# Moving four modulation items from the GDN heads to VectorE in the attention, with the gate's sigmoid on ScalarE

## What is computed

```python
c_act = jax.nn.silu(c)
for i in range(DEPTH):                                   # DEPTH = 2
    ada = (c_act @ ada_w[i] + ada_b[i])[:, None, :]      # 1 x 6144: six items
    sh1, sc1, g1, sh2, sc2, g2 = jnp.split(ada, 6, axis=-1)
    h = rms_norm(x) * (1.0 + sc1) + sh1
    y = gdn_mixer(h, ...) if i == 0 else fox_mixer(h, ...)
    x = x + g1 * y
    h = rms_norm(x) * (1.0 + sc2) + sh2
    x = x + g2 * hier_moe(h, ...)
return rms_norm(x, final_norm)

# fox_mixer, per head: q, k normalised; s = q k^T / 8 + cum_q - cum_k, causal
p = softmax(where(mask, s, -inf)); o = p @ v
o = o * jax.nn.sigmoid(g_out)
return o @ w_out
```

## Time and profile before

| | us |
|---|---|
| median of 3 runs (lowest, highest) | 1465.35 (1463.05, 1469.11) |
| profiled execution, its own time | 1467.78 |
| its span in the trace | 1466.2 |
| TensorE busy | 1337.1 (91% of the span) |
| VectorE, ScalarE, GpSimd busy | 731.8, 435.3, 397.0 |
| heads 1 to 6, 128.68 to 421.84 | 293.2 |
| attention, eight pairs, 854.3 to 1113.2 | 258.9 |

### The profile page before, as it was taken

One profiled execution on the slowest core, in us unless ns is written; L12 is line 12 of the kernel. 1 busy time (PEld: TensorE's weight loads), 2 busy tenths in 40 slices (PEclk: granted clock), 3 DMA queues, 4 the chain that ended last, 5 costly groups with the idle time before them and its releaser, 6 DMA issues.

```text
span 1466.2 us, 24949 instructions
## 1 busy us (share of the span) xinstructions
PE 1337.1 (91%) x9111; PEld 859.8 (59%) x9111; DVE 731.8 (50%) x1520; ACT 435.3 (30%) x1033; POOL 397.0 (27%) x588
## 2 busy tenths in 40 slices
PE   4999999999999989999886999999999979999881
PEld 2677767777775455555442777777764545555440
DVE  3656566667652466522223445666654557322224
ACT  4434424434442110000002645555541200000002
POOL 3022022112230023444334054434410024344320
PEclk8899999999999989999898899999999999999996
DMA  8255554512154279999997222122046379999995
GB/s 360 115 208 201 215 213 177 197 59 115 58 222 131 114 263 405 418 418 419 421 420 319 90 88 73 73 80 108 26 191 239 154 277 415 421 419 418 419 398 200
DMA packets 56693, 350.27 MB, mean 239 GB/s; under 512 B 18408, under 2 KB 18880, under 8 KB 30992
## 3 DMA queue, kind: packets, MB, share of 16 engines
q1 hardware_dynamic: 44992, 332.02, 57.1%
q0 software_dynamic: 11520, 16.83, 3.1%
q10 hardware_dynamic: 80, 0.04, 0.0%
HBM read 342.45 MB, written 27.34 MB: 252 GB/s over the span
## 4 chain that ended last, share of the span: by engine, by line
PE 70%; DMA 15%; DVE 9%; issue 2%; ACT 2%; POOL 1%; SPq 0%; POOLq 0%; DVEq 0%; ACTq 0%
PE PS L1116 10%; PE PS L771 8%; DMA hT<-in_moe_w_down_dram 8%; PE PS L773 7%; PE PS L772 7%; PE PS L1059 6%; PE PS L1123 5%; DMA Dr<-in_ada_w_dram 4%; PE PS L749 2%; PE PS L1143 2%; PE PS L1133 2%; PE PS L862 2%; PE PS L908 2%; PE PS L1108 2%; PE PS L1294 2%
## 5 line engine op out<-in xcount | busy, mean ns | idle before, releaser
L771 PE MATMUL PS<-hHi,Whi 128*128 128x512 f32 x512 | 225.3, 440 | 2.5 <-DVE hLo L1789 2.4
L773 PE MATMUL PS<-hHi,Wlo 128*128 128x512 f32 x512 | 202.8, 396 | 0.0
L772 PE MATMUL PS<-hLo,Whi 128*128 128x512 f32 x512 | 202.0, 394 | 0.0
L1360 ACT COPY arena<-PS 128x512 f32<-128x512 f32 (+4 forms) x256 | 108.6, 440 | 281.9 <-PE PS L862 104.7
L1116 PE MATMUL PS<-Wr,arena 128*64 128x256 f32 x1408 | 165.4, 389 | 9.8 <-DVE arena L2195 9.8
L1583 ACT ACTIVATE arena<-PS 128x128 f32<-128x128 f32 x72 | 20.0, 278 | 464.9 <-PE PS L1116 369.0
L1116 PEld LDWEIGHTS PS<-Wr,arena 128*64 128x64 f32 x1408 | 101.5, 140 | 88.8 <-issue 29.0
L2477 POOL DMA_INDIRECT y_rows<-arena x72 | 77.0, 1070 | 258.5 <-DVE arena L2207 252.2
L2418 POOL TENSOR_TENSOR Wlo<-Wr,Whi (+1 forms) x72 | 94.0, 1324 | 178.7 <-ACT Whi L1360 178.7
L771 PEld LDWEIGHTS PS<-hHi,Whi 128*128 128x128 f32 x512 | 97.6, 191 | 33.8 <-issue 18.2
L2201 DVE TENSOR_TENSOR arena<-arena,PS 128x128 f32<-128x128 f32 x72 | 20.7, 288 | 185.6 <-ACT arena L1583 169.0
(11 more groups left out here) (394 smaller groups left out, 2301.6 us busy)
## 6 DMA issues: line engine op xcount, KB each, us to landing
Wr<-in_moe_w_gate_up_dram SPq DMA_DIRECT2D x52, 2048.0 KB
Dr<-in_ada_w_dram SPq DMA_DIRECT2D x42, 1024.0 KB, 26.8
Dr<-in_moe_w_down_dram SPq DMA_DIRECT2D x28, 1024.0 KB
arena<-in_moe_w_gate_up_dram SPq DMA_DIRECT2D x14, 2048.0 KB
hT<-in_moe_w_down_dram SPq DMA_DIRECT2D x26, 1024.0 KB
Wr<-in_gdn_w_dram SPq DMA_DIRECT2D x8, 2048.0 KB, 8.6
Wr<-in_fox_w_dram SPq DMA_DIRECT2D x8, 2048.0 KB, 8.1
shift_scale<-in_moe_w_down_dram SPq DMA_DIRECT2D x12, 1024.0 KB
```

Of the source, the lines that this page charges most:

```text
L771: mm(out_ap, a_hi, b_hi, start=(k == 0), stop=False)
L772: mm(out_ap, a_hi, b_lo, start=False, stop=False)
L773: return mm(out_ap, a_lo, b_hi, start=False, stop=(k == KD - 1))
L1360: return nc.scalar.copy(dst, src)
```

## The change

`ADA_HEADS` becomes 3: two items in each of the heads 0 and 1, item 6 in head 2, item 7 in the last head. Items 8 to 11 (`LATER` = 8) are made in the attention, as eight *halves* of 512 numbers. For one half SP makes four loads of 512 KB into the part of `Dr` that the attention doesn't use, in two buffers; VectorE multiplies by `c` and adds up, in eight products over 128x512 (`later_products`); TensorE sums over the partitions in four matmuls with ones into PS[7]; VectorE adds the bias (`later_item`), and SP stores the result (`later_store`). The products of half 0 stand ahead of the attention; those of half p+1 stand in pair p, two in each query tile, the first of them ahead of the first tile's `pn_ok`. The gate is now e^(-ln(1+e^-g)), two ScalarE instructions behind the copy of v; VectorE's L2348 and L2349 are gone, and ScalarE's take of the gate doesn't wait for `sgt_ok` any more. New semaphore names stand for old semaphores that go on counting.

```diff
-ADA_HEADS = 5
+ADA_HEADS = 3
+LATER = 2 + 2 * ADA_HEADS
...
+        later_w = [Dr[:, 1, a * 1024:a * 1024 + 1024].rearrange("p (k c) -> p k c", k=2) for a in range(2)]
+        later_acc = ada_acc[:].rearrange("p i c -> p (i c)")
+        later_made = ada_bias[:, 0, 0:P]
...
@@ SP, sublayer_rows and experts
                 if layer == 1:
                     sp.wait_ge(wo_ok, WO)
+                    sp.wait_ge(later_out, 16 * 6 + later_dma_from)
...
                 if layer == 0:
+                    sp.wait_ge(ada_out[1], 16 * ADA_HEADS)
...
@@ SP, attention
+            def later_loads(m, at, quarters):
+                for q in quarters:
+                    if not isinstance(m, int) or m * KD + 2 * q - 2 > 0:
+                        sp.wait_ge(later_mul, m * KD + 2 * q - 2 + later_mul_from)
...
+                    later_load(*at, q)
...
+            def later_store(m, at):
+                sp.wait_ge(later_row, m + 1 + later_row_from)
...
+                load(later_half_row(ada_rows, *at), later_made[0:97:32, :], later_out)
+                sp.wait_ge(later_out, m * 16 + 16 + later_dma_from)
...
+            def later_step(m, at, then):
+                later_loads(m + 1, then, range(2))
+                later_store(m, at)
+                later_bias_load(then)
+                later_loads(m + 1, then, range(2, 4))
...
             bias_rows(0)
+            sp.wait_ge(modc_in, 32)
+            later_bias_load((LATER, 0))
+            later_loads(0, (LATER, 0), range(4))
             with sp.Fori(0, 3) as j:
                 for u in range(2):
                     pair_load(j * 2 + (2 + u), u, j * 2 + (1 + u))
                     bias_rows(j * 2 + (1 + u))
+                    later_step(j * 2 + u, (j + LATER, u), (j + (LATER + u), 1 - u))
             bias_rows(H - 1)
             sp.wait_ge(fpj_ps, 4 * 7)
             out_load(fox_w_out, 0, 0, mix_w[0])
+            later_step(H - 2, (11, 0), (11, 1))
             after_projection(1)
+            later_store(H - 1, (11, 1))
             sublayer_rows(1)
@@ TensorE, attend
                     pe.wait_ge(sqr_ok, p * 2 + (m + 1))
+                    if m == 0:
+                        if not isinstance(p, int) or p > 0:
+                            pe.wait_ge(later_row, p + later_row_from)
...
-                fill(2, 7)
+                fill(2, 5)
+                pe.wait_ge(fr_ok, p * 2 + 1)
+                pe.wait_ge(later_mul, p * KD + KD + later_mul_from)
+                for j in range(4):
+                    last = mm(PS[7][32 * j:32 * j + 32, 0:P], ones[:, 0:32], later_acc[:, j * P:j * P + P], start=True, stop=True)
+                last.then_inc(later_sum, 1)
+                fill(5, 7)
@@ ScalarE
-                    after(act, sgt_ok, p)
                     ins = A(eg, PS[1][:], ACT.Exp, scale=-1.0)
...
                 cp(vS.rearrange("p n c -> p (n c)"), PS[4][:]).then_inc(vs_ok, 1)
+                link(A(eg, eg, ACT.Ln, bias=one_ap))
+                after(act, on_ok, p)
+                A(sgate, eg, ACT.Exp, scale=-1.0).then_inc(sgt_ok, 1)
@@ VectorE
+            def later_products(m, k0, k1):
+                for k in range(k0, k1):
+                    if k % 2 == 0:
+                        dve.wait_ge(later_in[k // 2 % 2], m * 32 + (16 * (k // 4 + 1) + later_in_from[k // 2 % 2]))
+                    w = later_w[k // 2 % 2][:, k % 2, :]
+                    if k == 0:
+                        TS(later_acc, w, cact[:, 0:1], None, ALU.mult).then_inc(later_mul, 1)
+                    else:
+                        dve.wait_ge(later_mul, m * KD + k + later_mul_from)
+                        STT(out=later_acc, in0=w, scalar=cact[:, k:k + 1], in1=later_acc, op0=ALU.mult, op1=ALU.add).then_inc(later_mul, 1)
+            def later_item(p):
+                dve.wait_ge(later_sum, p + 1 + later_sum_from)
+                dve.wait_ge(later_bias, p * 16 + 16 + later_dma_from)
+                TT(later_made, PS[7][:, 0:P], later_made, ALU.add).then_inc(later_row, 1)
...
+                    if qt == 0:
+                        later_item(p)
+                    if more:
+                        later_products(p + 1, 2 * qt, 2 * qt + 1)
                     for a in range(2):
                         u = 2 * qt + a
                         dve.wait_ge(pr_ok, p * 8 + (u + 1))
...
+                    if more:
+                        later_products(p + 1, 2 * qt + 1, 2 * qt + 2)
                     if more and qt >= 2:
                         square_low(p + 1, qt - 2)
-                dve.wait_ge(fev, p * 4 + 4)
-                link(TS(eg, eg, 1.0, None, ALU.add))
-                nc.vector.reciprocal(sgate, eg).then_inc(sgt_ok, 1)
...
+            later_products(0, 0, KD)
             for m in range(2):
                 square_low(0, m)
             attend(0)
```

More of the change, by code:

```diff
@@ L417, in build @@
         on_ok = sem("on_ok")
+        later_in, later_in_from = (modc_in, cum_out), (32, 16)
+        later_mul, later_sum, later_row = osum_ok, sso_ps, s_ok
+        later_mul_from, later_sum_from, later_row_from = H, H, 3 * H
+        later_out, later_bias = ada_out
+        later_dma_from = 16 * ADA_HEADS
+        loop_passed = dve_passed
         r_ps, r_e, r_both, r_rank, r_pos, idx_ok = (sem(n) for n in ("r_ps", "r_e", "r_both", "r_rank", "r_pos", "idx_ok"))
@@ L564, in experts @@
                     sp.wait_ge(fs_ps, 2 * H)
+                    sp.wait_ge(later_mul, H * KD + later_mul_from)
                 for e in range(2):
@@ L576, in experts @@
                 sp.wait_ge(wo_ok, i * WO + 2 * NT)
+                if i == 1:
+                    sp.wait_ge(later_out, 16 * H + later_dma_from)
                 for g in range(2):
@@ L1699, in _ @@
             with act.Fori(0, 2) as j:
-                link.enter(j, 4)
+                link.enter(j, 6)
                 pair_step(j * 2 + 2, 0, j + 2)
@@ L2357, in _ @@
             with dve.Fori(1, H - 1) as p:
-                link.enter(p - 1, 17)
+                link.enter(p - 1, 16)
                 attend(p)
```

11 lines of the change are left out of this document (added).

## The result

| | us |
|---|---|
| before, median beside the change | 1467.23 (1463.05 to 1470.16) |
| changed kernel, median of 4 runs | 1518.83 (1513.39 to 1519.32) |
| ratio, 95% interval | 1.0332 (1.0298 to 1.0365) |
| profiled execution after, and its span | 1513.39, 1511.6 |

The account below looks back on a forecast made before the run. TensorE was taken as the bound in heads and attention; 38.6 us lost (5.5 + 0.5 + 18.5 + 9 + 0.6 + 1.5 + 3) less 16.8 gained gave +21.8, so 1487 us on the median, range 1468 to 1503.

Parts of the forecast that it names:

- the price of a loop pair: Pairs 1 to 5: VectorE's first product waits for its load, 3.7 us a pair, 18.5 in all; bounds 1.2 and 5.2.
- the start: Start of the attention: half 0's loads and eight products delay the low squares, TensorE 5.5 us late; bounds 4 and 8.
- The heads: Heads 2, 3 and 4 lose 16 matmul groups: 16.8 us gained, or 14.4 if load waits come up again.
- Pair 6: The load of half 7 stands behind 2 MB of `fox_w_out`: 9 us lost, bounds 7 and 11.
- The clock behind the two long stalls: Start and pair 6: the clock may fall to 1.2 GHz behind them, 3 us together, bounds 0 and 4.
- `modq`: Behind the last pair: its load waits for the last half's store, 1.5 us lost, bounds 0 and 4.
- The 3.5 us stalls I take as too short.: Pairs' first-tile stalls: claimed too short to lower TensorE's clock, so no clock loss was counted there.
- rival (c): Every stall lowers the clock, 2 us more in five pairs, and longer chains: 1497 to 1503 us, chance 0.14.
- I take 0.3 a pair.: TensorE's four sums over the partitions in each pair: 0.2 to 0.4 us, taken as 0.3.
- I give them 0.2 us a pair, for the third one.: VectorE's seven products behind the first in a pair: 0.2 us, for the third, whose tile has little slack.
- rival (d): Products take 1.77 us beside GpSimd, 9 us more over pairs 1 to 6: 1496 us, chance 0.08.
- it lands at 932.5: Pair 2: the first load, behind bias rows issued at 927.65, lands at 932.5; VectorE waits 2.2 us.

Follow-up runs that it names:

- e4: The kernel before with only the gate's sigmoid moved to ScalarE, no item moved: 1466.9 us, ratio 0.9995.
- e3: The changed kernel with three unread matmuls ahead of TensorE's first-tile wait in every pair: 1515.0 us, ratio 1.0307.
- e8: The changed kernel with half 0's loads issued ahead of the cumulative sums and its products split round VectorE's copy: 1512.1 us, ratio 1.0329.
- e10: The changed kernel with loads early, products moved into VectorE's idle time, each half's second load behind the pairs' weights: 1461.9 us, 0.9959 of the kernel before.

## Why the prediction was wrong

The step that failed is the price of a loop pair: 3.7 us forecast, with bounds of 1.2 and 5.2, and 7.5 measured, 19 of the 23.6 us by which the sum of this execution was short. Its largest part is the clock behind the pairs' stalls, which the prediction put at nothing. The second is the start, 5.5 forecast and 11.3 measured. The path itself was right.

**What held.** The bound and the mechanism: TensorE waits for VectorE in the first tile, and VectorE for a load of `Dr` that goes out behind the bias rows. The heads (15.9 us in heads 1 to 7, forecast 16.8). The bias rows go out 6.84 us behind the weights (930.74 against 923.90), the forecast's 927.65 - 920.64 = 7.01. VectorE has the item done at 933.91, 9.3 us into the pair, where the forecast had 8.9. ScalarE's gate at no cost (e4). Pair 6: TensorE idle for 8.21 us and 10.4 lost, forecast 9 and a share of the clock. The clock behind the two long stalls: TensorE worked 3.2 and 3.8 us at 0.50 behind them, which loses 3.5, forecast 3. The last pair, 0.4 against 0.6. `modq`, put at 1.5, cost nothing that the trace shows: TensorE's first instruction behind the last pair had no wait. The 1.1 us behind it lie within the 351.1 to 354.2 that this stretch took in all these traces.

**What failed.**

1. *"The 3.5 us stalls I take as too short."* The stalls came out at 4.0 to 4.3 us, and behind each TensorE worked at half clock, for 3.4 us or, in pair 4, 4.9. This cost 1.9 us a pair in the mean (1.8 by e3): 9.3 of the 23.6 us. It was rival (c), whose price of 2 us was right and whose chance was put at 0.14. The rows gave no ground for "too short". The 4 us of the earlier trace rows are the length of the window, and the wait in that place was 5.25:

```profile
758.39 1.03 PE L1143 MATMUL PS<-Dr,arena 128*32 128x512 f32 x1 [5.25 <-DMA hT<-in_moe_w_down_dram]
```

   That said what one longer wait does and nothing about 3.5. In e3 the clock fell even in pairs where TensorE's last idle stretch was only 1.64 and 1.81 us.
2. *The start, "5.5 us".* It was 11.3. The forecast had the first load there 4.9 us after the bias rows' issue, and then two more round trips of 3.3 us. In the trace the first product runs 6.85 us after that issue (834.46 against 827.61), the third pair of products at 840.57, some 4.3 us after the products that free its buffer, and the last pair at 845.18. Its load went out at about 838.1, the end of the first four products, and took 7.0 us: right behind it, at 839.07, SP sent the 2 MB of weights, which the forecast had nowhere beside it. The first load's 1.9 us and the last one's 3.7 make up nearly all of the difference of 5.8. That the last is due to the weights is not shown by a run made for it. It fits e8, where the same quarter has no weights right behind it and lands after 5.2.
3. *TensorE's sums: "I take 0.3 a pair."* By e10 a pair in which nothing is late is 0.93 us longer than before, so this was 0.6 too little, 3 us over the five pairs.
4. *"I give them 0.2 us a pair, for the third one."* TensorE waited 0.64 to 0.79 there. In pairs 2, 4 and 5 the product ahead of that tile's reciprocals takes 1.84 us instead of 0.75 (949.35), while GpSimd makes a low half at the same time:

```profile
949.36 1.29 POOL L2510 TENSOR_TENSOR Wlo<-Wr,Whi  x1 [4.87 <-ACT Whi L1428]
951.15 1.28 POOL L2510 TENSOR_TENSOR Wlo<-Wr,Whi  x1 [0.50 <-ACT Whi L1428]
```

   The scaling behind it, at 951.30, takes 1.34, where the next one takes 0.42 (952.75). In pairs 1 and 3 the product stays at 0.75, and both scalings are stretched in its place, with the same wait for TensorE. In pair 1:

```profile
908.77 0.75 DVE L2402 SCALAR_TENSOR_TENSOR ada_acc<-Dr,cact,ada_acc 128x512 f32<-128x512 f32 x1
909.63 1.26 DVE L2436 TENSOR_SCALAR arena<-arena 128x384 f32<-128x384 f32 x1
911.00 1.37 DVE L2436 TENSOR_SCALAR arena<-arena 128x384 f32<-128x384 f32 x1
```

   So a product there delays the tile by more than its own 0.75, whichever instruction GpSimd's work falls on. In the kernel before the first of these scalings took 0.95 already. This is rival (d) in one of its places. In the other place, the first product, it holds in part: 0.95 to 1.11 us in pairs 1 to 3, 0.48 and 0.49 in pairs 4 and 5. And the 1.77 us of the earlier trace rows, which the prediction called the far bound, is the median of L2320. The Trainium skill, GPSIMD Engine Reference, Specifications, names contention with GpSimd for instructions of VectorE with two SBUF inputs, which the product is. The trace agrees for it, with 1.84 against 0.75. The scaling has only one tensor as input and is stretched as well. That sentence of the skill also names a two-port mode, and no run here tells whether it applies.
5. *The first load of a pair, "it lands at 932.5".* That is 4.85 us after the bias rows' issue; the product that needs it started 6.1 us after it in pair 2 (936.86 against 930.74) and 7.0 in pairs 4 and 5, so 1.3 to 2.1 us later than forecast. The forecast's 3.5 held 0.3 of TensorE's own sums and started from the 0.17 of before, so a wait of 3.4; TensorE waited 4.1 in the mean. The price came from the earlier trace rows, where no other large load was issued close by. SP also needs 0.6 to 0.7 us to issue one such load (1.46 for two, at 931.44), against 0.34 for the bias rows.

By pair: 0.93 of own work, 4.10 in the first tile less the 0.17 of before, 0.75 in the third, 1.9 of clock: 7.5, which is what was measured. Of pair 0's 2.8, own work (0.9) and the clock behind the start (1.6) are 2.5.

The range failed too. By the prediction's own prices (c) and (d) together give at least 1487 + 10 + 9 = 1506, so its high end of 1503 holds either of them and not both, and nothing was left for later landings or for a start beyond its bound of 8. Bounds that stem from the same belief, that loads land as they do when alone, have to move together. No run shows whether a stall of 3.5 us would keep the clock.

## What to carry to other kernels

A load that is put in a queue in program order has to be priced with everything that is sent just ahead of it and just behind it, and not with its landing time when alone: here 512 KB took 5.5 us in the median and up to 10.3, against 3.3. When a change puts a new wait of some us on the critical path, price the work behind it at both clock levels, unless a trace has a wait of that length behind which the clock stayed up. And where work moves to an engine with idle time, look where in the loop this idle time is: the same products and loads made this kernel 3.3% slower in one order and 0.4% faster in another.
